# Expert down tiles of steps 0 to 5 issued by ScalarE on its own DMA queue

## The reference

```
def swiglu(h, wg, wu, wd):
    return (jax.nn.silu(h @ wg) * (h @ wu)) @ wd

logits = h @ w_router ; top_v, top_i = top_k(logits, 2) ; gate = softmax(top_v)
for e in range(8):
    out = out + comb[..., e:e + 1] * swiglu(h, wg[e], wu[e], wd[e])
```

## Time and profile before

| what | us |
|---|---|
| median of three runs | 1609.54 |
| the profiled execution, its own time | 1610.84 |
| its span, first to last instruction | 1608.9 |
| PE busy in the span | 1583.3 (98%) |
| DVE, ACT, POOL busy | 747.3, 594.1, 43.2 |
| mean granted TensorE clock | 0.995 |

### The profile page before, as it was taken

How to read it: one execution, slowest core, us unless ns; L and a number is a source line. 1 busy time by engine, 2 the same in 40 slices (tenths; PEclk the granted TensorE clock), 3 DMA queues, 4 the chain that set the end, 5 groups by cost and what they waited for, 6 DMA issues and landing times.

```text
span 1608.9 us, 35813 instructions
## 1 busy us (share of the span) xinstructions
PE 1583.3 (98%) x16105; PEld 1367.8 (85%) x16105; DVE 747.3 (46%) x910; ACT 594.1 (37%) x821; POOL 43.2 (3%) x63
## 2 busy tenths in 40 slices
PE   8999999999999999999999999999999999999997
PEld 7778888888887888988888888888888898888885
DVE  5757556666676654343332333433333333342344
ACT  6644443434565432232323323223223232232323
POOL 1000000000000000000000000000000000000010
PEclk9999999999999999999999999999999999999999
DMA  8524335455442547999999999999999999999961
GB/s 332 210 104 159 131 120 205 182 209 190 183 190 95 194 158 284 382 380 404 386 375 392 375 374 396 382 376 382 395 372 382 386 392 376 390 377 378 389 263 68
DMA packets 39480, 471.22 MB, mean 293 GB/s; under 512 B 4480, under 2 KB 4752, under 8 KB 9776
## 3 DMA queue, kind: packets, MB, share of 16 engines
q1 hardware_dynamic: 35280, 454.33, 71.5%
q0 software_dynamic: 3632, 13.58, 2.8%
q10 hardware_dynamic: 432, 1.19, 0.2%
HBM read 463.18 MB, written 5.90 MB: 292 GB/s over the span
## 4 chain that ended last, share of the span: by engine, by line
PE 92%; DMA 3%; DVE 3%; ACT 1%; issue 1%; POOL 0%; POOLq 0%; DVEq 0%; SPq 0%; ACTq 0%
PE PS L1412 22%; PE PS L1409 13%; PE PS L851 12%; PE PS L853 11%; PE PS L852 11%; PE PS L1140 9%; PE PS L1141 4%; PE PS L1369 1%; DMA stage<-wm_dram 1%; DMA w1v<-wl_dram 1%; PE PS L1202 1%; PE PS L1182 1%; PE PS L923 1%; DMA xs<-mem_dram 1%; DVE wlo L1487 1%
## 5 line engine op out<-in xcount | busy, mean ns | idle before, releaser
L1412 PE MATMUL PS<-ring,e_in 128*32 128x128 f32 x5376 | 597.4, 273 | 0.0
L1409 PE MATMUL PS<-ring,e_in 128*32 128x384 f32 x5376 | 589.2, 487 | 0.0
L1412 PEld LDWEIGHTS PS<-ring,e_in 128*32 128x32 f32 x5376 | 582.4, 110 | 0.0
L1981 DVE TENSOR_TENSOR wlo<-stage,whi 128x2048 fp32r<-128x2048 f32 x110 | 247.1, 2288 | 218.8 <-ACT whi L748 218.8
L748 ACT ACTIVATE whi<-stage 128x2048 fp32r<-128x2048 f32 x110 | 204.4, 1906 | 141.1 <-DMA stage<-wm_dram 141.1
L1409 PEld LDWEIGHTS PS<-ring,e_in 128*32 128x32 f32 x5376 | 214.3, 109 | 8.0 <-issue 7.9
L1487 DVE TENSOR_TENSOR wlo<-stage,whi 128x2048 fp32r<-128x2048 f32 (+2 forms) x56 | 176.3, 3150 | 93.3 <-ACT whi L469 93.3
L787 ACT ACTIVATE a_hi<-PS 128x288 fp32r<-128x288 f32 x112 | 30.9, 328 | 486.0 <-PE PS L1369 486.0
L2059 DVE TENSOR_TENSOR a_lo<-PS,a_hi 128x288 fp32r<-128x288 f32 x112 | 34.8, 352 | 323.3 <-ACT a_hi L787 323.3
L851 PE MATMUL PS<-whi,a_hi 128*96 128x512 f32 x448 | 181.5, 405 | 2.4 <-DVE wlo L1981 2.4
L469 ACT ACTIVATE whi<-stage 128x2048 fp32r<-128x2048 f32 (+2 forms) x57 | 148.3, 2606 | 94.5 <-PE PS L853 52.1
(11 more groups left out here) (350 smaller groups left out, 1662.1 us busy)
## 6 DMA issues: line engine op xcount, KB each, us to landing
ring<-wm_dram SPq DMA_DIRECT2D x112, 2048.0 KB, 12.5
stage<-wm_dram SPq DMA_DIRECT2D x56, 2048.0 KB, 10.1
stage<-wl_dram SPq DMA_DIRECT2D x20, 2048.0 KB, 7.9
stage<-wf_dram SPq DMA_DIRECT2D x33, 1024.0 KB, 4.8
stage<-wl_dram SPq DMA_DIRECT2D x4, 1816.0 KB, 8.4
w1k<-wl_dram SPq DMA_DIRECT2D x2, 2048.0 KB, 8.1
w1v<-wl_dram SPq DMA_DIRECT2D x2, 2048.0 KB, 8.0
third<-wl_dram SPq DMA_DIRECT2D x2, 1816.0 KB, 9.0
```

What stands on the lines that cost most here:

```text
L1409: mm(bank(kind)[rows, 0:3 * P], e_in[:, k, rows], w[:, k, 0:3 * P], start=(k == 0), stop=(k == KD - 1), skip_group_check=True)
L1412: ins = mm(bank(kind)[CAP:P, t * P:(t + 1) * P], e_in[:, k, t * PIECE:(t + 1) * PIECE], w[:, k, 3 * P:4 * P], start=(k == 0 and t == 0), s ...
L1981: V.tensor_tensor(wlo[2][:, half], stage[2][:, half], f32(whi[2][:, half]), ALU.subtract).then_inc(w_lo[2] if part else half_lo, 1)
```

## The change

SP no longer issues the down tiles of steps 0 to 5 (other than the very first tile of item 0); ACT does, right behind its silu of the same step, after waiting for `w_lo[2]`. The sixth step's down tile (index 6, the last of an item) stays with SP, behind the gate ring tile of that step, and so do the first down tile of all and the last, which goes to another buffer. ACT's loop over items now reads the item's expert number into a register at its start.

```diff
                     load_up(e, p)
                     s = (p - RING) // 2
-                    if p % 2 and not (first and s == 0):
+                    if s == -1 and p % 2:
                         sp.wait_ge(w_lo[2], it * MOE_STEPS + (s + MOE_FILLS[2]))
-                        load_down(e if s >= 0 else e_before, s % MOE_STEPS, 2)
+                        load_down(e_before, MOE_STEPS - 1, 2)
...
             load_down(last, MOE_STEPS - 1, 0)
-            for s in (4, 5):
-                sp.wait_ge(w_lo[2], n_items * MOE_STEPS + (s - MOE_STEPS + MOE_FILLS[2]))
-                load_down(last, s, 2)
...
+            def load_down(it, e, s):
+                act.wait_ge(w_lo[2], it * MOE_STEPS + (s + MOE_FILLS[2]))
+                act.dma_start(stage[2][:], wm_d[bass.ds(e, 1), s, 2, :, :].rearrange("o p n -> p (o n)")).then_inc(w_in_ring[2], 16)
+
+            def item(it, e, first=False):
...
                     nc.scalar.activation(hid_tok[:, 0, :], bank(0)[:, 0:3 * P], ACT.Silu).then_inc(f_silu, 1)
+                    if not begin and s < MOE_STEPS - 1:
+                        load_down(it, e, s)
...
             with act.Fori(1, n_items) as it:
-                item(it)
+                item(it, act.value_load(items_i[0:1, bass.ds(it, 1)], min_val=0, max_val=E - 1))
```

More of the change, by code:

```diff
@@ L788, in turned_hi @@
                 ins.then_inc(ma_hi, 1)
-            def item(it, first=False):
+            def load_down(it, e, s):
+                act.wait_ge(w_lo[2], it * MOE_STEPS + (s + MOE_FILLS[2]))
+                act.dma_start(stage[2][:], wm_d[bass.ds(e, 1), s, 2, :, :].rearrange("o p n -> p (o n)")).then_inc(w_in_ring[2], 16)
+            def item(it, e, first=False):
                 for s in range(MOE_STEPS):
@@ L817, in item @@
                     nc.scalar.activation(hid_tok[:, 0, :], bank(0)[:, 0:3 * P], ACT.Silu).then_inc(f_silu, 1)
-            item(0, first=True)
+                    if not begin and s < MOE_STEPS - 1:
+                        load_down(it, e, s)
+            item(0, 0, first=True)
             act.wait_ge(items_ready, 1)
```

## The result

| | median us | lowest to highest | runs |
|---|---|---|---|
| before | 1608.62 | 1606.62 to 1610.57 | 4 |
| after | 1670.43 | 1668.29 to 1678.71 | 4 |

The ratio is 1.0388, with a 95% interval of 1.0357 to 1.0418: 3.9% slower, +61.8 us. The forecast was slower, 1645 in a range of 1604 to 1680. The time lies in the range and the mechanism is the one forecast, but the loss is 1.7 times the forecast one.

The account below looks back on a forecast made before the run. PE was taken to set the time, with DMA almost full (0.97) and down tiles tight. 1610.84 + 39.6 for 36 stalled steps - 4.1 at the start gave 1646.3 profiled, so 1645 us, range 1604 to 1680.

Parts of the forecast that it names:

- Issue time, ACT and SP cost nothing: At the issuing engines: ACT's wait and issue (0.35 us) are hidden, SP's earlier issues gain 0; all taken as 0.
- The queue makes the down tile land with the third tile: In the DMA queues: tiles share by halves, the down tile ending last of three, 18.9 us after the gate issue.
- A fresh stall of 2.2 us: At PE's second half of a down tile: split ends at 25.35, wanted at 23.14, a shortfall of 2.2 us.
- 36 steps, and nothing in the others: Of 47 tiles from ACT, 7 behind SP's tiles and about 4 at the ends lose nothing, leaving 36.
- 1.1 us a step: In counted steps: a stall shortens the next, so two lose 2.2 us together; the bounds were 0.4 and 1.95.
- No clock loss in the likeliest case: In the expert stage's stalls: the 1645 us case had 0.4 to 1.3 us a step without half clock; chance 0.62.
- a rival at 1675: In the expert stage: each stall also halves PE's clock for a while, 1.95 us a step; chance 0.12.
- The start gains 4.1 us: At the stage's second down tile: landing 5.6 us sooner removes a 2.4 us stall and 1.7 us of clock loss.
- The sum: Whole kernel: 1610.84 + 39.6 - 4.1 = 1646.3 us for a profiled execution, so 1645 for the median.
- Nothing moves: Whole kernel: same issue times, bytes and engines; 1609.5 us if the first stall stays too; chance 0.10.
- Only the start is won: In the expert stage: the loop keeps step and only the 4.1 us at its start show, 1605.4 us; chance 0.16.
- ACT was not held up: Rival at ACT's semaphore: a late split keeps ACT waiting while the turned tile waits; some us, no chance given.

Follow-up runs that it names:

- The wait alone: Kernel before, with ACT waiting for w_lo[2] behind its silu in steps 0 to 5 while SP still issues all tiles; 1609.47 us, ratio 0.9998.
- the kernel with three tiles in ACT's queue: Kernel before, with ACT issuing gate, down and up tiles in steps 0 to 2, gate and down in step 3; SP has the rest; 1634.01 us, 1.0148.
- the next one: ACT issues all tiles of steps 0 to 2 and step 3's gate tile; step 3's down tile is back with SP, ahead of the up tile; 1614.30 us, 1.0029.
- the last one: Kernel before, with ACT issuing down and up tiles in steps 0 to 2 and SP the gate tile and steps 3 to 6; 1608.01 us, 1.0002.
- the mirror image: Kernel before, with all down tiles from SP and ACT issuing the ring tiles of steps 0 to 3; 1659.01 us, 1.0317.
- the one-tile kernel: Kernel before, with only the down tile of step 3 of each item issued by ACT; 1629.92 us, 1.0120.
- the two-tile kernel: Kernel before, with the down tiles of steps 2 and 3 of each item issued by ACT; 1637.92 us, 1.0174.
- three quarters: Changed kernel, with ring tiles of items 1 to 7 loading 3072 of 4096 columns; 1641.46 us, 1.0189.
- its own experiment: Kernel before, with only item 0's second down tile issued by ACT; 1607.15 us against 1609.97, ratio 0.9994.
- The kernel with the split's hold: Changed kernel, with SP holding each up ring tile until DVE's multiply, right behind the split; 1675.99 us, 1.0387.

## Why the prediction came out as it did

**Issue time, ACT and SP cost nothing: right.** The wait alone gave 0.9998. SP's freed time gained nothing either.

**The queue makes the down tile land with the third tile: right, and shown.** The landings are 11.9 us (11.5 to 13 were forecast). That it is the up tile in another queue was shown by one tile's place: down tile in ACT's queue and up tile in SP's (step 4 of the kernel with three tiles in ACT's queue), down tile moved to the up tile's queue with the rest at its place (the next one), and both in ACT's queue (the last one). The other explanations fell: ACT's waits, SP's hold at the split, ACT as the issuer (the mirror image), and the gate tile or the changes of queue (the last one). What the full engines do is smaller than I thought: at a share of 0.82 half of the loss was still there.

**A fresh stall of 2.2 us: right.** One tile alone gave 2.44 at the mean of eight, 2.2 without clock; the eight are far apart, 0.9 to 4.2 us.

**36 steps, and nothing in the others: this is the term that failed.** That 36 steps are longer is luck. I had put 11 of the 47 tiles at nothing: the seven behind a tile that stays with SP, where the loop starts fresh, and four in the first and last steps. The seven are used in step 1 of items 1 to 7, and all seven of these steps are longer, 10.5 us together without clock. A fresh loop doesn't spare its first tile: in the one-tile kernel such a tile had the whole 2.2 us. The four (I take steps 2 and 3 of item 0 and 5 and 6 of item 7) lost 2.8 us, in item 0. In their place nine of the steps that I had counted in are not longer, six of them step 6, which is 17.54 us long and so has 0.9 us more room. So 13.3 of the 55.5 us lie in steps that the forecast had put at nothing. (PE waits 49 times in the 36 steps, since it waits for the first half of the split too.)

**1.1 us a step: right as a mean.** The 36 steps that I had counted in lost 42.2 us without clock, 1.17 each, where 39.6 were forecast; over all 47 it is 1.18. It is 1.54 only if the steps that lost nothing are left out. I had halved the fresh stall on the ground that a stall takes its length off the next one. Two tiles in a row bear that out (1.4 times the loss of one, not twice), and so does the mean, but not step by step: without clock steps 1 to 5 lost 1.5, 1.2, 1.0, 1.1 and 2.2 us, and step 6 nearly nothing. Step 5 stands out, as it did with three quarters (+1.74), and POOL's gather (`xg`) is in flight with its down tile. That the gather makes the difference is argued from the place alone. It stays open.

**No clock loss in the likeliest case: wrong in part.** 8.5 us were lost. I had this as a rival at 1675 in which each second stall halves the clock; four stretches in 36 longer steps did. My forecast was for one end of a thing that lies between.

**The start gains 4.1 us: the gain came, and was spent.** Step 2 of item 0 won 3.9 us, and alone in its own experiment it stayed won. In the changed kernel the next tile's stall (+4.1 us, with half clock) took it back.

**The sum.** For the profiled executions: 55.5 us of stalls where 39.6 were forecast, 8.5 of clock where none was, 4.3 of before gone as forecast (4.1), and a start of the stage 2.1 earlier, which isn't the change's (in all traces but one this copy starts between 655.7 and 659.0 us): +57.6, beside 57.4 measured in the span and 35.5 forecast. The medians are 61.8 apart, since the profiled execution was the fastest of the four after and slower than the median of those before.

**The rivals.** "Nothing moves", with the rule of the Trainium skill behind it ("DMA: Bandwidth & Descriptors", section "Rules for kernel authors": spreading over issuing engines gives no bandwidth), fell by 3.9%. The rule is true of the bandwidth, which didn't rise (358 GB/s in the stretch of 708 us, 383 before), but says nothing of the order of landing, and that is where the time went. "Only the start is won" fell with the 49 waits. ACT was not held up: the copies to a_hi are behind the waits for PE alone.

## What to carry to other kernels

A tile with little slack should be in the same queue as the tile that is issued beside it and has much slack, and ahead of it: in this kernel the tight tile then had the engines to itself, and in two queues it landed when both had. What a second queue costs can be read from the trace before: take the tight tile's landing, add the service time of the tile that would share with it, and compare with the slack (10.1 + 4.95 = 15.05 us here, and 15.1 in the step shown of the one-tile kernel, against a slack of 2.4 us). Look for it too where the DMA share is well under 1: at 0.82 half of the loss was there. When counting the tiles that will stall, don't leave out the one behind a fresh start: nothing has put off PE's need for it yet.

## What the runs showed of the hardware that I had not expected

- A tile in a queue of its own started late while the other queue was busy: none of its packets in the 3.5 us behind its issue, against 91 of the other queue, then 20 against 27 and 124 against 131. Over the eight tiles that ACT issued in the one-tile kernel the first packet came after 1.5 to 3.5 us; of the tile of the earlier trace rows, with nothing beside it, after 1.0.
- With 0.82 of the engines' time in use the same order of issue still cost 1.9%.
- Only the longest idle pieces of PE cost clock: 40.6 us of waits in 49 pieces led to four stretches at half clock, with the four longest idle pieces (2.5 to 3.1 us). The kernel with the split's hold, with 35 waits of up to 3.9 us and six other idle pieces of up to 6.2, had seven such stretches, 37.5 us in all, and so lost up to 18.8 us. It isn't the length alone: pieces of 2.1 and 2.2 us had a stretch at half clock in the two-tile kernel, and one of 2.4 us had none.
